# Expert outputs added into gathered residual rows instead of a separate output stage, in an encoder block on eight cores

## What is computed

```
h = h + merged @ w_out
u = rmsnorm(h, norm2_g)
group  = argmax of 4 group logits of u          (one group)
e1, e2 = the 2 best of the 8 experts of it      (gates p1, p2, each with the group's probability)
h = h + p1 * ffn_e1(u) + p2 * ffn_e2(u)         ffn: silu(u @ w_gate) * (u @ w_up), @ w_down
out = rmsnorm(h, final_g)
```

## Time and profile before

| | |
|---|---|
| median of 3 runs | 1487.23 us (1483.15 to 1489.48) |
| the profiled execution, its own time | 1493.79 us |
| its span on the slowest core (7) | 1492.2 us |
| spans of the cores | 1464.0, 1452.1, 1453.8, 1463.7, 1469.8, 1488.1, 1480.8, 1492.2 us |
| busy share of the span: PE, DVE, ACT, POOL | 71%, 59%, 50%, 20% |
| last chain of work by engine | PE 45%, DVE 18%, issue 14%, ACT 8%, DMA 8% |

### The profile page before, as it was taken

How to read it: one execution, slowest core, us unless ns; L and a number is a source line. 1 busy time by engine, 2 the same in 40 slices (tenths; PEclk the granted TensorE clock), 3 DMA queues, 4 the chain that set the end, 5 groups by cost and what they waited for, 6 DMA issues and landing times.

```text
span 1492.2 us, 23009 instructions; the slowest of 8 cores (1452.1 to 1492.2 us)
## 1 busy us (share of the span) xinstructions
PE 1066.1 (71%) x6606; PEld 546.1 (37%) x6606; DVE 879.3 (59%) x1812; ACT 738.9 (50%) x1387; POOL 305.6 (20%) x316
## 2 busy tenths in 40 slices
PE   2589667788888889999848999968547777776000
PEld 1345223333333334444423444424334544453000
DVE  3434699899999999999811344334632322322186
ACT  5733656677777778888743222235313323332132
POOL 2025402122121212221221000022123333332000
PEclk9999577889999999999988999989759998899555
DMA  9402554575868679999676220081237889985592
GB/s 195 113 1 29 63 58 58 71 97 74 97 72 98 81 83 108 112 105 104 90 97 136 30 29 1 1 296 50 85 109 247 274 270 293 288 297 174 190 350 107
DMA packets 76322, 187.73 MB, mean 126 GB/s; under 512 B 18792, under 2 KB 30568, under 8 KB 72096
## 3 DMA queue, kind: packets, MB, share of 16 engines
q0 software_dynamic: 51264, 87.55, 39.6%
q1 hardware_dynamic: 20320, 86.05, 18.8%
q10 hardware_dynamic: 4608, 12.58, 2.1%
HBM read 223.33 MB, written 88.08 MB: 209 GB/s over the span
## 4 chain that ended last, share of the span: by engine, by line
PE 45%; DVE 18%; issue 14%; ACT 8%; DMA 8%; another core or an unknown queue 3%; POOL 2%; DVEq 0%; ACTq 0%; SPq 0%; POOLq 0%
DVE R L961 9%; PE ps L1214 7%; PE ps L1608 5%; PE ps L1632 4%; DMA R<-y_rows 3%; PE ps L823 3%; PE ps L1020 2%; PE ps L1021 2%; PE ps L1038 2%; PE ps L1314 2%; PE ps L1039 2%; PE ps L623 2%; PE ps L1198 2%; PE ps L1206 2%
## 5 line engine op out<-in xcount | busy, mean ns | idle before, releaser
L961 DVE TENSOR_SCALAR_CACHE_REDUCE R<-R 128x272 bf16<-128x272 f32 (+14 forms) x240 | 342.2, 1426 | 11.6 <-DVE R L961 0.5
L1024 ACT ACTIVATE R<-ps,R 128x512 bf16<-128x512 f32 x304 | 209.1, 690 | 70.4 <-PE ps L1021 63.8
L813 ACT ACTIVATE R<-ps 128x400 bf16<-128x400 f32 (+14 forms) x352 | 159.3, 512 | 55.0 <-PE ps L808 53.5
L1038 PE MATMUL ps<-R 128*128 128x512 bf16 x304 | 120.2, 395 | 36.1 <-ACT R L1046 34.4
L1050 POOL TENSOR_TENSOR R<-R 128x512 bf16<-128x512 f32 x32 | 40.6, 1270 | 455.6 <-ACT R L1048 357.7
L1020 PE MATMUL ps<-R 128*128 128x512 bf16 x304 | 121.2, 399 | 7.4 <-DVE R L928 3.9
L823 PE MATMUL ps<-R 128*128 128x400 bf16 (+14 forms) x352 | 105.7, 379 | 26.1 <-POOL R L796 16.4
L1021 PE MATMUL ps<-R 128*128 128x512 bf16 x304 | 120.7, 397 | 0.0
L1039 PE MATMUL ps<-R 128*128 128x512 bf16 x304 | 120.2, 395 | 0.0
L1214 PE MATMUL ps<-R 128*128 128x512 bf16 x512 | 116.9, 382 | 0.0
L808 PE MATMUL ps<-R 32*128 32x400 bf16 (+14 forms) x352 | 71.9, 370 | 30.9 <-DVE R L928 14.9
(11 more groups left out here) (210 smaller groups left out, 1854.3 us busy)
## 6 DMA issues: line engine op xcount, KB each, us to landing
R<-expert_bf SPq DMA_DIRECT2D x32, 1024.0 KB
R<-x SPq DMA_DIRECT2D x32, 512.0 KB
expert_bf<-w_eg POOLq DMA_DIRECT2D x32, 512.0 KB, 12.1
expert_bf<-w_eu POOLq DMA_DIRECT2D x32, 512.0 KB
expert_bf<-w_ed POOLq DMA_DIRECT2D x32, 512.0 KB
R<-expert_bf SPq DMA_DIRECT2D x32, 512.0 KB
R<-y_rows SPq DMA_DIRECT2D x16, 1024.0 KB
out<-R ACTq DMA_DIRECT2D x16, 512.0 KB, 5.2
```

The costliest lines, as they stand in the source:

```text
L813: pg.op('act', lambda e, bx=bx, ri=ri: e.activation(out=rbuf[ri][:, 0:n], in_=banks[bx][:, 0:n], func=AF.Relu), reads=[PB[bx]], writes=[B( ...
L961: pg.op('dve', lambda e: e.tensor_scalar(out=junkbf[:, 0:S], in0=sc[:, 0:S], scalar1=mids[:, n_ - 1:n_], scalar2=None, op0=ALU.is_ge, op1= ...
L1024: pg.op('act', lambda e: e.activation(out=pT[pi], in_=banks[bl][:, 0:512], func=AF.Exp, scale=ATTN_SCALE, bias=negsh[:, par:par + 1]), rea ...
L1038: e.matmul(banks[bO][:, 0:512], lhsT=ckeys[:, i, 0:128], rhs=pT[pi], start=first, stop=last_)
```

## The change

The residual moves to a table `h_rows` in HBM (2048 rows of 1024 numbers and the two gates, `HW` = 1026), and each expert adds its weighted result to gathered rows of it:

- In the join stage `hacc` is replaced by a ring of eight tiles `xr`; ACT also stores each tile to `h_rows`. `x` is loaded a tile an iteration; `xn2` has four buffers. Expert 0's weights load before the stage, those of 1, 2 and 3 in it.
- `expert_at`: experts go as 0, 8, 16, 24, 1, 9, ...: groups in turn, so that the two experts of a pair share no token, nor do two neighbouring pairs. Lists mark the choice that comes second for its token (`sec`) and which gate is meant (`kk`).
- Before the expert stage: `probs`, a store of the gates to the last two columns of `h_rows`, more index arithmetic, first gathers.
- In it, `pull_h(i)` gathers three tiles of `h_rows`; it waits for the scatters of pair i-2. `weigh` picks the gate (two small DVE operations). Each of the four products is added by DVE from PSUM to the gathered row with its gate. `settle` squares and sums the row on ACT and scatters it back to `h_rows` (rows in their first expert; others have an index out of bounds). At every second expert ACT takes three roots, and `spread_out` scales the row on DVE and scatters it to `out` (rows in their second expert).
- `y_rows`, `fetch`, `merge`, `leave` go. Six weight buffers for four; DMAs under way 12, 12 and 20.

```diff
-NDS = 32
-POOLS = {'sp': (0, 12), 'act': (12, 8), 'pool': (20, 12)}
+NDS = 44
+POOLS = {'sp': (0, 12), 'act': (12, 12), 'pool': (24, 20)}
...
+        walk = list(range(NT))
+        w_offs = [('R2', 0), ('R0', 0), ('R0', 12288), ('R1', 0), ('R2', 16384), ('R1', 12288)]
+        def expert_at(x_):
+            return 8 * (x_ % 4) + x_ // 4
...
+                pg.dma('act', hrow_d[128 * j:128 * (j + 1), 0:D], xr[s], reads=[B('xr', s, 0), B('xr', s, 1)],
+                       writes=[B('h_row', j)])
...
+                if t + 6 < NT and t >= 2:
+                    load_x(t + 6)
+                if t == 4:
+                    load_w(2)
+                if t == 8:
+                    load_w(3)
...
+        def pull_h(i):
+            for q, col in ((0, 2 * i), (1, 2 * i + 1), (2, 32 + i)):
+                n = 3 * (i % 4) + q
+                al = [] if i > 3 else xrs if n < 7 else late_r3
+                pg.gather(hr[n], hrow_d, idx_g[:, col:col + 1], TX - 1,
+                          reads=[B('idx_g'), B('pp_row')] + hrows + [B('h_upd', i % 2, q_) for q_ in range(3)],
+                          writes=[B('hr', n, 0), B('hr', n, 1)] + al)
...
+        def spread_out(n, col, o):
+            pg.op('dve', lambda e: e.reciprocal(out=sq3[:, col:col + 1], in_=sq3[:, col:col + 1]),
+                  reads=[B('sq3', col)], writes=[B('sq3', col)])
+            pg.op('dve', lambda e: e.scalar_tensor_tensor(
+                out=ob[o], in0=hr[n][:, 0:D], scalar=sq3[:, col:col + 1], in1=gbc[0], op0=ALU.mult, op1=ALU.mult),
+                reads=[B('hr', n, 0), B('hr', n, 1), B('sq3', col), B('gbc', 0)], writes=[B('ob', o)])
+            pg.scatter(out_d, idx_o[:, col:col + 1], ob[o], TX - 1, reads=[B('idx_o'), B('ob', o)], writes=[B('out', col)])
+        def settle(n, col, q, i):
+            o = obc[0] % 5
...
+            pg.op('act', lambda e: e.activation(out=ob[o], in_=hr[n][:, 0:D], func=AF.Square,
+                                                accum_out=sq3[:, col:col + 1]),
+                  reads=hb, writes=[B('ob', o), B('sq3', col)] + first)
+            pg.scatter(hrow_d, idx_h[:, col:col + 1], hr[n], TX - 1, reads=[B('idx_h')] + hb,
+                       writes=[B('h_upd', i % 2, q)])
...
-                    if hh == 0:
-                        pg.op('act', lambda e, bk=bk, y=y, lo=lo, hi_=hi_: e.copy(
-                            out=y[lo:hi_, 0:512], in_=banks[bk][lo:hi_, 0:512]), reads=[PB[bk]], writes=[yb] + al)
-                    else:
-                        pg.op('dve', lambda e, bk=bk, y=y, lo=lo, hi_=hi_: e.tensor_copy(
-                            out=y[lo:hi_, 512:1024], in_=banks[bk][lo:hi_, 0:512]), reads=[PB[bk]], writes=[yb] + al)
+                    pg.op('dve', lambda e, bk=bk, hh=hh, n=n, col=col, lo=lo, hi_=hi_: e.scalar_tensor_tensor(
+                        out=hr[n][lo:hi_, 512 * hh:512 * (hh + 1)], in0=banks[bk][lo:hi_, 0:512],
+                        scalar=gk[lo:hi_, col:col + 1], in1=hr[n][lo:hi_, 512 * hh:512 * (hh + 1)],
+                        op0=ALU.mult, op1=ALU.add),
+                        reads=[PB[bk], B('gk', col), B('hr', n, hh)], writes=[B('hr', n, hh)])
...
+            fresh = []
+            if 0 < x_ <= N_EXP:
+                fresh = project(x_ - 1)
+                if x_ - 1 + NWB < N_EXP:
+                    load_d_w(x_ - 1 + NWB)
+            if x_ % 2 == 1 and x_ // 2 + 1 < N_EXP // 2:
+                pull_h(x_ // 2 + 1)
+            owed += fresh
+            if x_ % 2 == 0 or x_ > N_EXP - 1:
+                for n, col, o in owed:
+                    pg.op('act', lambda e, col=col: e.activation(out=sq3[:, col:col + 1], in_=sq3[:, col:col + 1], func=AF.Sqrt,
...
+                for a_ in owed:
+                    spread_out(*a_)
+                owed = []
```

More of the change, by code:

```diff
@@ L1235, in build @@
         reset('R2')
-        xg = [[carve_at('R2', 2048 * (3 * i + q), BF16, [P, D]) for q in range(3)] for i in range(2)]
+        xg = [[carve_at('R0', xt_off + 2048 * (3 * i + q), BF16, [P, D]) for q in range(3)] for i in range(2)]
         cursor['R2'] = 12288
@@ L1257, in build @@
+        cursor['R3'] = 33088
+        sec = carve('R3', F32, [P, 48])
+        kk = carve('R3', F32, [P, 48])
+        nk = carve('R3', F32, [P, 48])
+        pp = carve('R3', F32, [P, NT, 2])
+        sq3 = carve('R3', F32, [P, 48])
+        gk = carve('R3', F32, [P, 48])
+        xn2 = [carve_at('R0', 24576 + 2048 * i, BF16, [P, D]) for i in range(4)]
+        uTs = [carve_at('R1', 24576 + 2048 * i, BF16, [P, KC, 128]) for i in range(2)]
         t32 = carve_at('R0', junk_off, F32, [P, D])
-        sqj = carve_at('R3', 32768, BF16, [P, D])
+        sqj = carve_at('R1', 28672, BF16, [P, D])
@@ L1292, in build @@
             pg.dma('sp', rconst, croute_d, writes=[B('rconst')])
-            for j in list(range(8, 12)) + list(range(0, 8)):
-                load_x(j)
-            load_w(0)
             load_w(1)
@@ L1447, in ranks @@
                     if g == 1:
-                        for j in range(NH, NT):
+                        for j in range(NH):
                             e.matmul(rkb, lhsT=ones_m, rhs=mk_ap(hot, 32 * j, [[pstep(hot), 128], [0, NH], [1, 32]]),
@@ L1566, in build @@
         pg.branch_on(flag[0:1, 0:1], [B('flag')])
+        pg.dma('sp', gbc[0], gf_d.partition_broadcast(128),
+               writes=[B('gbc', 0)] + [B('ohx', k_, g) for k_ in range(2) for g in range(2)])
         hidm = [carve_at('R0', 29184 + 768 * i, BF16, [P, 2, CAP]) for i in range(3)]
@@ L1569, in build @@
         xTm = [carve_at('R3', 3072 * i, BF16, [P, KC, CAP]) for i in range(4)]
-        ysb = [carve_at('R3', 12288 + 4096 * i, F32, [P, D]) for i in range(5)]
-        early = [B('xn2', k) for k in range(2)] + [B('uTs', k) for k in range(2)]
-        late_r3 = [B('R3a')]
+        early = [B('xn2', k) for k in range(4)]
         def turn(i):
@@ new lines, in weigh @@
+        def weigh(n, col):
+            hb = [B('hr', n, 0), B('hr', n, 1)]
+            pg.op('dve', lambda e: e.tensor_scalar(out=gk[:, col:col + 1], in0=hr[n][:, D + 1:D + 2], scalar1=kk[:, col:col + 1],
+                                                   scalar2=None, op0=ALU.mult), reads=hb + [B('kk')], writes=[B('gk', col)])
+            pg.op('dve', lambda e: e.scalar_tensor_tensor(
+                out=gk[:, col:col + 1], in0=hr[n][:, D:D + 1], scalar=nk[:, col:col + 1], in1=gk[:, col:col + 1],
+                op0=ALU.mult, op1=ALU.add), reads=hb + [B('nk'), B('gk', col)], writes=[B('gk', col)])
@@ L1653, in build @@
+            return done
         turn(0)
-        for x_ in range(N_EXP + 1):
-            if x_ == 8:
-                probs()
+        owed = []
+        for x_ in range(N_EXP + 2):
             if x_ < N_EXP:
                 expand(x_)
-                if x_ + 4 < N_EXP:
-                    load_gu_w(x_ + 4)
+                if x_ + NWB < N_EXP:
+                    load_gu_w(x_ + NWB)
             if x_ % 2 == 0 and x_ // 2 + 1 < N_EXP // 2:
@@ L1721, in build @@
         rowb = [carve_at('R0', xt_off + 2048 * i, BF16, [P, D]) for i in range(4)]
+        hacc = carve_at('R1', 0, F32, [P, NT, D])
+        for j in range(NT):
+            pg.dma('sp', hacc[:, j, :], hrow_d[128 * j:128 * (j + 1), 0:D], reads=[B('h_row', j)],
+                   writes=[B('hacc', j, 0), B('hacc', j, 1)])
         for j in range(NT):
```

258 lines of the change are left out of this document (130 added, 128 removed).

## The result

The changed kernel takes 1627.4 us (median of 4 runs, 1619.24 to 1628.83) against 1486.2 of the kernel before beside it: a ratio of 1.093, 95% interval 1.086 to 1.099. Forecast were 1458 us and a range up to 1503. It is 141 us slower, and outside every case that the prediction named. The times that follow are medians of all executions, and the ratios compare those in which no die was held back by a lower clock; where one die is behind in nearly all executions no ratio was formed, and the dies are given instead.

What follows compares the result with a forecast made beforehand. Data (DMA) was taken to set the expert stage's pace. First expand at 1100, plus 15 paces of 22.5, minus 8, plus 34 gave an end of 1463.5, 28.7 earlier; from the median 1487.2 that is 1458 us, range 1408 to 1503.

Steps and rivals of the forecast that it cites:

- Output stage, -117 and a tail of 34: Output stage goes, 117 us of the span; from the last pair's first expand to the end about 34 us.
- the next time 0: End of the last evacuation of a pair's second expert; forecast 7 us after the last pair's first expand.
- Join stage, -16 and +3: Join stage: four xn2 buffers and less x loaded ahead save 16 us; h_rows stores and ACT's copy add 3.
- the join stage gains nothing, since the new stores take the place of the loads: Rival on the join stage: no gain there, forecast +16, 1474 us; chance 0.06.
- `probs`, the gates' store and the first gathers of `h_rows` lie beside the landing of the `u_rows` gathers: Ahead of the expert stage: these overlap the u_rows landings; only +2 us was counted for routing.
- The pace, 22.5: Expert stage: a pair's operations followed in order give 20.7 us, plus 1.4 for clock and 0.4 for waiting; 22.5 taken.
- The clock, 0.8 at 60%: Expert stage: PE clock taken as 0.8 with PE busy 60%, adding 1.4 us a pair.
- DMA as a limit: Expert stage: 5.77 MB a pair take 20.7 us at 279 GB/s; rival that DMA alone sets the pace, 1428 us, chance 0.25.
- A sixteenth of the h traffic more for unaligned rows: h_rows transfers: rows starting 8 bytes further into a 256-byte block take one transaction more, adding a sixteenth of h traffic.
- If the generator splits them, an issue could cost more: POOL in the expert stage: splitting 4104-byte h_rows rows could at most double issue cost, 28 us a pair.
- The scatter that feeds the gather: Rival, expert stage: pull_h waits for pair i-2's landings; at 15 and 20 us, pace 25.5, time 1503 us; chance 0.20.
- Table drain: Rival, ACT's table loads: a drain of about 1.38 us each, pace 1.4 longer, time 21 us more; chance 0.04.

Runs made afterwards that it cites:

- theory C: Theory formed after the result: POOL's gathers issued in a row hold up what TensorE releases, on one die.
- the gathers apart: row_alias with u_rows gathers behind a pair's two h scatters and h_rows gathers behind its three scatters to out: 1510.0 us, ratio 1.018.
- row_alias: The changed kernel with 4160-byte rows, where only the first h gather into each of two regions names the buffers it takes over: 1561.8 us.
- theory A: Theory formed after the result: rows of 4104 bytes make every store, gather and scatter of h_rows dear.
- before_pull_far: The kernel before with u_rows gathers behind a pair's scatters, two pairs ahead of their transposes, into a third set of buffers: 1496.1 us, ratio 0.999.
- late_root: The gathers apart with a pair's roots and scalings one expert later and h_rows gathers right behind those of u_rows: 1495.6 us, 1521.0 a second time.
- late_root_spread: late_root with u_rows gathers moved behind the next pair's first scatter, 1.5 pairs ahead of their transposes, h_rows gathers kept: 1557.2 us (1517 to 1593).

## Why the prediction was wrong

The profiled execution's slowest core, 3, against the sum: the first `expand` at 1137.2, forecast 1100; from there to the first `expand` of the last pair 433.3 us, forecast 329.5; from there to the end 47.2, forecast 34. So 37 us were lost ahead of the expert stage, 104 in its pace and 13 behind it. The step that failed most is the pace of a pair, 28.6 us on this die instead of 22.5, which lacked the wait of theory C; the second is the join stage, 22 us longer than before where 13 less were counted.

What each mending gave, by the dies of the profiled executions: rows of 4160 bytes 72 us on one die and 41 on the other, the aliases 16 and 25, the gathers apart 0 and 41. By the medians of all executions the die behind has 52, 16 and 46. That leaves 1474 and 1504, against 1463.5 in the sum. The runs were made on more than one chip, and the die behind moves by some 30 us between executions, so its figures are rough.

- *Output stage, -117 and a tail of 34*: the stage is gone, but what comes in its place was 12 to 13 us too small (47.2 on core 3, 45.7 on core 6 of row_alias). The walk ended at the landing of the last scatter. In the trace some 10 us pass from the last bytes of the stores to `out` to the end of the span (1607.8 to 1617.7), with no instruction shown on any engine. The kernel before has the same (1481.8 to 1492.2 on core 7), and the sum put this at nothing. The rest is the way to "the next time 0": 9 to 10 us, not 7.
- *Join stage, -16 and +3*: wrong for this kernel. "If they delay `xn2` again, the gain shrinks": they did, by theory A, and the stage took 117 us by the median instead of 95. With aligned rows the term is right: 84 us, 11 less than before where 13 were forecast, and the first `expand` comes at 1098, 7 us earlier than before (forecast 11). So the rival "the join stage gains nothing, since the new stores take the place of the loads" had the wrong reason: with aligned rows the same stores leave most of the gain.
- *"`probs`, the gates' store and the first gathers of `h_rows` lie beside the landing of the `u_rows` gathers"*: wrong twice. The store of 2048 pieces of 8 bytes took 19.9 us, and POOL stood still until it had landed. The dependencies of the h gathers, which stand in the diff, were not read: `al` makes a chain of landings.
- *The pace, 22.5*: the walk was right, to 0.2 us on the die without the wait (22.3 in row_alias, 22.4 late in the change itself). It lacked the 7 us on the other die. The wait was in the earlier trace rows, 4.24 and 4.11 us, and the text read it as data that came late: "its pace is set by data", with 16.9 us needed for 17.1 measured as the proof. before_pull_far moves the same data with little of this wait, and the other die of the kernel before moves it in 14.8 us a pair. That two numbers agreed within 1% hid the cause, and they had to agree: 279 GB/s is what this core moved at this pace, so bytes divided by it give the pace back, whatever sets it. The 12.7 us "near the end, when the gathers and nearly all weight loads are over" was the place that tells the two apart, and the right reading was the first half of that sentence.
- *The clock, 0.8 at 60%*: close. Core 6 of row_alias has 0.84 from 1150 to 1350 with PE busy 0.59; core 3 of the change 0.76 from 1200 to 1530 with 0.54.
- *DMA as a limit*: the engines moved 202 GB/s at 0.67 on core 3, and 258 at 0.77 on core 6 of row_alias at the pace of 22.3. They were not the bound, and the 279 GB/s taken as one were not a limit: 324 on core 0 of the kernel before.
- *A sixteenth of the h traffic more for unaligned rows*, an estimate from the rule of the Trainium skill (DMA: Bandwidth & Descriptors, How a descriptor splits into AXI transactions): far too little here. The join stage's engine time per byte went up by 341/199 = 1.7, with the stores to `h_rows` about a third of the bytes. If the rest kept its rate, the stores into rows of 4104 bytes took some three times the time of aligned ones; an estimate from the two windows.
- *"If the generator splits them, an issue could cost more"*: it didn't. A gather of `h_rows` takes POOL 1.00 us, like one of `u_rows`.
- *The scatter that feeds the gather*, the slower rival: it priced landings at 15 and 20 us. On core 4 the medians from 1200 to 1530 were 5.8 for the scatters and 7.0 for the gathers. It hardly came, and its 1503 was too low for what came.
- *Table drain*: none, again: the load starts at 1422.43, takes 1.28, and the root starts at 1423.73.

The range failed because each unknown was given an end from a row of before, and none of these rows had an odd pitch or six gathers in a row.

## What to carry to other kernels

Choose the pitch of a table in DRAM before anything else: eight bytes too many cost this kernel 40 to 70 us, and padding to a multiple of 32 gave them back. Read a wait with no releaser against the same place in a pair where one suspect is missing and against the other die of the same execution, and look at what every other engine does when it ends. Where a new buffer takes over old ones, let one transfer carry the dependency; a list of aliases on each makes them a chain.

## What the hardware showed that was not expected

- Rows that start off a multiple of 32 bytes cost time, not packets: 199 GB/s per busy engine time with a pitch of 4104 bytes against 341 with 4160 and 330 with 4128, at the same 87,864 packets of the whole run. The gates' store of 2048 pieces of 8 bytes took 19.9 us to land, with pieces of 64 bytes on aligned rows 4.6. In that store both the length of the pieces and their place changed, and the runs don't tell the two apart.
- On one die of a chip, what TensorE releases reaches ACT and DVE late while POOL issues indirect DMAs in a row: 4.1 us with three gathers, 7 with six, up to 13.6 in late_root and 13.8 in late_root_spread. In the rows shown the first three end 1.2 to 2.1 us after the last gather has ended, the fourth does not. The other die doesn't show it. On each of the three chips that ran several kernels the same die was behind in all that had the wait, on two of them die 1, on one die 0. That the wait follows the place of the gathers is shown by the runs that moved them. How the release is held up, and how many DMAs in a row it takes, they don't show.
